# Moving the weight slots, the normed columns and the arena so that the two operands of a split product start 32 bytes apart, modulo 256

## The reference, cut to what matters

```python
def swiglu(x, w_gate, w_up, w_down):
    return (jax.nn.silu(x @ w_gate) * (x @ w_up)) @ w_down

x = x + 0.5 * rms_norm_2(swiglu(rms_norm_2(x, ng[0]), w_gate, w_up, w_down), ng[1])
h = rms_norm_2(x, ng[2])
```

## Time and profile before

| | |
|---|---|
| median of three runs | 3295.79 us (3285.26 to 3297.68) |
| profiled execution | 3285.75 us, of which the span of instructions is 3283.9 us |
| mean granted TensorE clock | 0.94 of 2.4 GHz |
| TensorE matmul busy | 2854.2 us, 87% of the span, 17,520 instructions |
| weight loads busy | 2248.3 us, 68% |
| VectorE busy | 2441.1 us, 74% |
| DMA | 868.24 MB, mean 264 GB/s |

### The profile page before, as it was taken

How to read it: one execution, slowest core, us unless ns; L and a number is a source line. 1 busy time by engine, 2 the same in 40 slices (tenths; PEclk the granted TensorE clock), 3 DMA queues, 4 the chain that set the end, 5 groups by cost and what they waited for, 6 DMA issues and landing times. The chain is left out here.

```text
span 3283.9 us, 44518 instructions
## 1 busy us (share of the span) xinstructions
PE 2854.2 (87%) x17520; PEld 2248.3 (68%) x17520; DVE 2441.1 (74%) x4651; ACT 771.0 (23%) x1993; POOL 618.8 (19%) x520
## 2 busy tenths in 40 slices
PE   8999987777777889877777777999998999998899
PEld 8889853333333789533333325999887999997898
DVE  7455687777776886877777767878747878877786
ACT  4322222222222343222222222011323001023300
POOL 0000034444444100344444441000000000000000
PEclk9999998888998999988888888999999999999899
DMA  6454699999999637899999996665204666652464
GB/s 211 147 172 155 212 377 419 416 410 419 408 402 421 230 104 237 341 419 417 419 415 399 407 421 253 195 202 162 68 28 154 192 204 185 207 184 87 135 195 148
DMA packets 471089, 868.24 MB, mean 264 GB/s; under 512 B 18912, under 2 KB 399712, under 8 KB 403168
## 3 DMA queue, kind: packets, MB, share of 16 engines
q0 software_dynamic: 73728, 536.90, 39.6%
q1 hardware_dynamic: 396864, 328.24, 31.6%
q10 hardware_dynamic: 288, 0.24, 0.0%
HBM read 855.89 MB, written 9.44 MB: 264 GB/s over the span
## 5 line engine op out<-in xcount | busy, mean ns | idle before, releaser
L2834 PE MATMUL banks<-arena,arena 128*128 128x512 f32 x1744 | 911.6, 681 | 315.7 <-ACT arena L2911 315.7
L2834 PEld LDWEIGHTS banks<-arena,arena 128*128 128x128 f32 x1744 | 370.4, 219 | 838.5 <-issue 448.9
L2792 POOL DMA_INDIRECT arena<-in_peer_uv,arena x512 | 613.8, 1199 | 1310.9 <-PE banks L2834 636.5
L3069 DVE CUSTOM_DVE_ANT_0 arena<-arena,normed 128x1024 f32<-128x1024 f32 x512 | 625.8, 1223 | 226.8 <-DMA arena<-in_peer_uv,arena 224.2
L457 DVE TENSOR_TENSOR weight_ring_part<-weight_ring,weight_high_parts 128x2048 fp32r<-128x2048 f32 (+3 forms) x243 | 537.6, 2212 | 8.3
L3623 PE MATMUL banks<-normed_columns_part,weight_high_parts 128*128 128x256 f32 x1408 | 394.1, 280 | 2.9 <-DVE weight_ring_part L457 2.4
L3624 PE MATMUL banks<-normed_part,weight_high_parts 128*128 128x256 f32 x1408 | 391.8, 278 | 0.0
L3625 PE MATMUL banks<-normed_columns_part,weight_ring_part 128*128 128x256 f32 x1408 | 391.6, 278 | 0.0
L454 DVE CAST weight_high_parts<-weight_ring 128x2048 fp32r<-128x2048 f32 (+3 forms) x243 | 288.6, 1188 | 92.6 <-PE banks L930 64.9
L928 PE MATMUL banks<-weight_high_parts,arena_part 128*128 128x256 f32 x1200 | 337.3, 281 | 7.0 <-PEq L397 3.9
L929 PE MATMUL banks<-weight_ring_part,arena_part 128*128 128x256 f32 x1200 | 334.1, 278 | 0.0
(11 more groups left out here) (606 smaller groups left out, 4265.9 us busy)
## 6 DMA issues: line engine op xcount, KB each, us to landing
weight_ring<-in_ffn_w_gate SPq DMA_DIRECT2D x88, 512.0 KB, 3.7
weight_ring<-in_ffn_w_up SPq DMA_DIRECT2D x88, 512.0 KB, 4.9
weight_ring<-in_ev_w_in SPq DMA_DIRECT2D x33, 1024.0 KB, 5.5
weight_ring<-in_ffn_w_down SPq DMA_DIRECT2D x32, 1024.0 KB, 5.2
weight_ring<-in_od_w_in SPq DMA_DIRECT2D x23, 1024.0 KB, 5.3
weight_ring<-in_peer_wq SPq DMA_DIRECT2D x16, 1024.0 KB, 5.6
weight_ring<-in_xa_wkv SPq DMA_DIRECT2D x13, 1024.0 KB, 5.7
weight_ring<-in_ev_w_out SPq DMA_DIRECT2D x12, 1024.0 KB, 5.4
```

Of the source, the lines that this page charges most:

```text
L2792: pool.indirect_dma_start(out=ring[:, slot(i, s), :], out_offset=None, in_=table, in_offset=bass.IndirectOffsetOnAxis(ap=index[:, i % 2, s ...
L2834: mm = pe.matmul(k.ps[:, 2 * b + half, :], diag[:, g % 2, s, :], v, start=n == b * PEER_TOPK, stop=n == last_mixed[b])
L3069: dve.tensor_tensor_reduce(out=ring[:, here, 0:D], in0=ring[:, here, 0:D], in1=k.xn[:, i % NB, :], scale=1.0, scalar=0.0, op0=ALU.mult, op ...
```

## The change

The slot grows by 16 floats to 2,096 floats (8,384 bytes, 192 more than a multiple of 256). `tile` works out the start in the slot from the buffer's own address, so that streamed weights start at 192 and loaded weights at 0 modulo 256. An unused tensor of 40 floats is put ahead of `normed`, and the arena gets 136 floats fewer, so that it still ends where the memory ends. Added up in the order of allocation this puts `weight_high_parts` at byte 58,240, `normed` at 100,064, `normed_columns` at 108,256 and `arena` at 116,448; the last three are 224 modulo 256. Loaded weights (0) are then 32 bytes behind streamed columns (224), and loaded columns (224) are 32 behind streamed weights (192). No instruction is added, removed or moved in any queue.

```diff
-ARENA = 28360
+ARENA = 28224
...
-SLOT = KC * WIDTH + LINE
+SLOT = KC * WIDTH + LINE + LINE // 2
...
         self.wide = sb("norm_scale_columns", [P, T])
+        sb("line_rest", [P, 40])
         self.xn = sb("normed", [P, NB, D])
...
     def tile(self, buffer, slot, n):
         kc, width = self.plan[n][0].shape[1], sum(src.shape[2] for src in self.plan[n])
-        at = LINE * ((slot + (0 if n in self.streamed else 1)) % 2)
+        home = self.place["weight_ring" if buffer is self.ring or buffer is self.ring_low else "weight_high_parts"]
+        at = ((192 if n in self.streamed else 0) - home - 4 * SLOT * slot) % 256 // 4
         return buffer[:, slot, at:at + kc * width].rearrange("p (c n) -> p c n", c=kc)
```

## The result

The change makes the kernel slower: 3321.2 us (3318.81 to 3322.06, four runs) against 3295.74 us (3285.26 to 3297.68), a ratio of 1.0088 with a 95% interval from 1.0073 to 1.0103. I had forecast 3257 us and a range that ended at 3312. The profiled execution after took 3320.42 us, its span is 3318.5 us; that is 34.6 us more than the span before. The medians differ by 25.5 us only: the execution that was profiled before the change lies some 10 us under the median of its runs.

A forecast was written before the change was run, and what follows sets the result against it. Gathers were taken to pace the expert layers and matmul cost nearly everything else. 19.0 plus 21.8 us from split products, 41 less 8 off the path, took 3285.75 to 3253; allowing for the median, forecast 3257, range 3244 to 3312.

The forecast's parts named there:

- What bounds the kernel: Gathers pace the two expert layers (1345 us); nearly everywhere else TensorE hardly rests, so the cost of a matmul sets the time.
- the floor of 111.7: Pitch in ns set by a 128-column load, taken from 200-column and plain float32 matmuls; 256-column split products were to reach it.
- the slow class: Stretches of 256-column split products at 117.9 ns pitch instead of 113.3; share put at 0.4 of all these matmuls.
- Rival 3: All split products: at 32 bytes behind, the load meets the stream earlier, 117.9 ns becomes the rule; +26 us, 3312; chance 0.16.
- Rival 1: Split products: the offset does nothing, both pitches come from how PE restarts after a wait; 3285 to 3298 us; chance 0.29.
- What changes a class: In gapless stretches of split products, a pitch once entered was said to stay until PE has to wait.
- The share off the path: Of 41 us gained, 8 would not count: 2 beside the gathers in expert layers, 6 waiting for VectorE in `columns_out`.
- rival 4: Expert layers: gathers land more slowly at a start that is a multiple of 32 only; up to 13 us; chance 0.05.
- The scatter: Runs may differ only in the share of 117.9 ns stretches, 0.22 being worth 10 us; without classes all reach 3253.

## Why the prediction was wrong

**What bounds the kernel** was read rightly. In the second stack a nanosecond on each split product came through almost whole: 27.7 us of slower products, 25.6 us of time.

**The failed step** is the bound that I chose for the pitch at the new offset: "I take the floor of 111.7, since the rows that stand nearest (the same load, the same kind of instruction, 200 columns) have it." The pitch came out at 118.3, just above the other end of the range that I had drawn (the slow class everywhere, 117.9). The experiments show why the row did not carry over. The 200-column tile passes through all eight multiples of 32 and keeps 112 ns, before and after; split products of 256 columns stand at 115 to 120 ns over the same eight. So the row of the shorter stream is not what is left of a 256-column product at a better distance: it tells only that there the distance does not matter. From one distance nothing could be read of the others, and the distance of before happens to be the best of those measured. The honest estimate was two-sided, with no reason to prefer the lower end.

**Rival 3 named the effect.** I gave it 0.16. Its place (every stretch of split products) and its price (26 us on the path, an end at 3312) were right: 25.6 us in the second stack and 2 us between the layers. Its reason is not shown. The pace is not the old slow class but one of its own, 0.5 ns slower, and that the load meets the stream earlier at a smaller distance does not give the order of the table, in which 160 is as bad as 0. "Nothing in the rows says that less distance is worse" was true, and nothing said the opposite.

**Rival 1 and the rule** from the Trainium skill, page "TensorE: Matmul & The Clock Gate", section "Part 2: What happens when you issue a matmul" (loading weights takes no read bandwidth from the running matmul), by which I let the offset be worth nothing: the runs refute it for this case. With nothing changed but addresses the mean pitch goes from 115.1 to 119.9 ns. Beside the 200-column stream they don't contradict it.

**What changes a class** I had read too narrowly. Rival 1 leans on a class that changes only when PE waits. The trace of before has at least four changes in which no two starts are more than 122 ns apart, each where loaded weights give way to loaded columns. One of them (a window as in the earlier trace rows, then start us, length us, instruction):

```profile
3193.00:3213.00 20.00, 20.00 (x179) 1.00 0.62 195
...
3213.15 0.28 PE L3625 MATMUL banks<-normed_columns_part,weight_ring_part 128*128 128x256 f32 x1
3213.27 0.28 PE L928 MATMUL banks<-weight_high_parts,arena_part 128*128 128x256 f32 x1
...
3218.80 0.28 PE L930 MATMUL banks<-weight_high_parts,arena_part 128*128 128x256 f32 x1
```

Up to there the pitch is 113.3 ns; from the first product with loaded columns on it is 117.7 over 47 pitches. The count of 11,856 split products, too, leaves out 48 (the trace has 11,904), which changes nothing.

**The share off the path** was too high. Of the loss none was taken up in the second stack beyond some 2 us; I had put a fifth off the path.

**The gathers** were rival 4, up to 13 us, with nothing in the forecast. In the two profiled executions the layers lost 7.9 us, and without these the span would have grown by 27 us, which is about the 26 of rival 3. But the split that I named, multiples of 64 against multiples of 32 only, is not the one that matters, and "a gain has no row that speaks for it" missed a gain of 14 us. With rows that start at 0 modulo 256 the two layers take 1283 to 1291 us together (three kernels); with the six other starts that were run (32, 64, 128, 160, 192 and 224) 1297 to 1309 (ten kernels), those at 64 and 128 among them, at 1298 and 1303. The Trainium skill has a rule on it, page "DMA: Bandwidth & Descriptors", section "How a descriptor splits into AXI transactions": a transaction begins at a multiple of 256 bytes, and a descriptor that starts off it begins with the bytes from the boundary below. The page tells this of bytes that are fetched; here it is the start of what is written that moved, and it is not said that the same holds there. If it does, an estimate from this page is 33 transactions for a row of 8 KB in place of 32, 3%. The landing went from 10.4 to 10.0 us, 4% (the two other kernels at 192 have 10.3 and 10.1), and the layers became 1.1% shorter. The sign agrees, and so does that 128 is no better than 192. That this is the cause was not tried apart. Between 192 and 224 the runs can't decide either: two other kernels with the ring at 192 took 1302 us in the layers, as against 1297 in the one before and 1305 after the change.

**The scatter.** I said that runs differ by the share of the slow class alone, and that with one class they would all come out alike. The changed kernel bears it out (3.3 us between its runs, beside 12.4), but the changed kernel with the ring moved has one class too, and its runs span 3297.5 to 3312.3 us. So part of the scatter has another source, which stays open.

What stays open is why 64 is the best distance, why two classes exist at 64 and 192, and what sets the choice between them there. No run tells that, nor was a distance tried that is not a multiple of 32 in all tiles at once.

## What to carry to other kernels

Where TensorE runs gapless with a new load for every 256 streamed columns, the relative start of the two operands was worth up to 4% of the mean pitch here (115.1 to 119.9 ns), the same in either role: measure all eight multiples of 32 bytes, and don't infer one from another or from a shorter stream. When memory is shifted for one user, look at what else lies behind the shift: moving the gather ring and the layer's tensors behind it so that the rows land on a multiple of 256 gave 0.38%, and on top of the change it took back half of the loss. If a stretch shows two paces, price the change both ways, from the faster and from the slower one.

## What was not expected of the hardware

- The pitch of a 256-column product with a new load depends on the distance of its two operands' starts modulo 256: from 113.3 ns at best (64) to 120.2 at worst (0), on average from 115.1 to 119.9; 8 bytes off 64 give 118.4 with loaded weights and 120.1 with loaded columns.
- The order over the distance is not monotone: 0 and 160 are the worst at 120, 128 and 32 stand between at 118.3 to 118.8, and 224 is better than both at 117.2.
- A gapless stretch can go from one pace to the other without a wait, where the two operands exchange their roles (113.3 to 117.7 ns).
- Indirect DMA of rows of 8 KB into SBUF lands in 9.9 to 10.0 us (median) in the three kernels with a start of 0 modulo 256, beside 10.1 to 10.7 in the other ten, with DMA busy 0.99 to 1.00 of the time before, after and with the moved ring.
